# Two thirds of a layer-modulation product moved from TensorE matmuls to VectorE multiply-adds, with a column of ones on TensorE for the sum over partitions

## The reference, cut to what matters

```python
...
"w_mod": n(ks[4], (DEPTH_2, D_MODEL, 3 * D_MODEL), 0.5 * D_MODEL ** -0.5),
"b_mod": n(ks[5], (DEPTH_2, 3 * D_MODEL), 0.02),
...
# per layer: silu(c) @ w_mod + b_mod, split in three of 2048: shift, scale, gate
```

## Time and profile before

| what | value |
|---|---|
| median of 3 runs | 2578.33 us (2578.1 to 2579.03) |
| profiled execution, first to last instruction (its span) | 2577.6 us |
| PE busy | 2556.3 us, 99% |
| DVE busy | 1702.8 us, 66% |
| ACT busy | 1274.2 us, 49% |
| DMA | 570.19 MB, mean 221 GB/s |
| granted TensorE clock | 0.999 of full |

### The profile page before, as it was taken

One profiled execution on the slowest core, in us unless ns is written; L12 is line 12 of the kernel. 1 busy time (PEld: TensorE's weight loads), 2 busy tenths in 40 slices (PEclk: granted clock), 3 DMA queues, 4 the chain that ended last, 5 costly groups with the idle time before them and its releaser, 6 DMA issues.

```text
span 2577.6 us, 31440 instructions
## 1 busy us (share of the span) xinstructions
PE 2556.3 (99%) x12416; PEld 2051.5 (80%) x12416; DVE 1702.8 (66%) x2467; ACT 1274.2 (49%) x1754; POOL 94.9 (4%) x142
## 2 busy tenths in 40 slices
PE   8999999999999999999999999999999999999998
PEld 6777777777777777788888888888888888888887
DVE  5555665664654444457688767598986765898866
ACT  6544544534534333345445565445655554455654
POOL 0000000000000000000100000020000000200000
PEclk9999999999999999999999999999999999999999
DMA  9776786776776777875655447744446666545454
GB/s 336 256 274 229 243 283 229 245 270 227 254 260 222 286 273 278 291 262 198 225 181 178 164 152 259 254 165 164 147 158 221 237 209 216 184 147 164 148 182 177
DMA packets 350594, 570.19 MB, mean 221 GB/s; under 512 B 18208, under 2 KB 202784, under 8 KB 346608
## 3 DMA queue, kind: packets, MB, share of 16 engines
q1 hardware_dynamic: 343216, 532.84, 60.3%
q0 software_dynamic: 6512, 34.60, 3.8%
q10 hardware_dynamic: 720, 0.75, 0.1%
HBM read 559.70 MB, written 8.42 MB: 220 GB/s over the span
## 4 chain that ended last, share of the span: by engine, by line
PE 95%; DMA 3%; ACT 1%; DVE 1%; issue 0%; POOL 0%; SPq 0%; DVEq 0%; ACTq 0%
PE acc L454 28%; PE acc L456 27%; PE acc L455 27%; PE aux L889 3%; PE aux L1094 2%; PE aux L1119 1%; DMA raw<-in_w_o 1%; PE aux L1236 1%; DMA raw<-in_w_mod 1%; PE aux L1104 1%; DMA xr_s<-c_mid 1%; DMA xr_s<-x_mid 1%; PE aux L751 1%; PE aux L1013 0%; PE aux L1074 0%; PE aux L766 0%
## 5 line engine op out<-in xcount | busy, mean ns | idle before, releaser
L442 DVE TENSOR_TENSOR w_lo<-raw,w_hi 128x1024 fp32r<-128x1024 f32 x808 | 993.3, 1233 | 730.9 <-ACT w_hi L434 730.1
L434 ACT ACTIVATE w_hi<-raw 128x1024 fp32r<-128x1024 f32 x808 | 848.6, 1059 | 909.9 <-PE acc L456 888.7
L454 PE MATMUL acc<-w_hi,h_hi 128*128 128x512 f32 x2240 | 892.6, 398 | 10.1 <-DVE w_lo L442 10.1
L456 PE MATMUL acc<-w_hi,h_lo 128*128 128x512 f32 x2240 | 874.3, 390 | 0.0
L455 PE MATMUL acc<-w_lo,h_hi 128*128 128x512 f32 x2240 | 873.3, 390 | 0.0
L454 PEld LDWEIGHTS acc<-w_hi,h_hi 128*128 128x128 f32 x2240 | 421.2, 188 | 124.6 <-issue 32.5
L456 PEld LDWEIGHTS acc<-w_hi,h_lo 128*128 128x128 f32 x2240 | 420.9, 188 | 89.7
L455 PEld LDWEIGHTS acc<-w_lo,h_hi 128*128 128x128 f32 x2240 | 421.6, 188 | 83.4
L454 PE MATMUL acc<-w_hi,u_hi 128*128 128x512 f32 x800 | 318.7, 398 | 0.4 <-DVE w_lo L442 0.4
L456 PE MATMUL acc<-w_hi,u_lo 128*128 128x512 f32 x800 | 312.1, 390 | 0.0
L455 PE MATMUL acc<-w_lo,u_hi 128*128 128x512 f32 x800 | 311.8, 390 | 0.0
(11 more groups left out here) (333 smaller groups left out, 1827.9 us busy)
## 6 DMA issues: line engine op xcount, KB each, us to landing
raw<-in_w_in SPq DMA_DIRECT2D x631, 512.0 KB, 4.5
raw<-in_w_mod SPq DMA_DIRECT2D x192, 512.0 KB, 7.3
raw<-in_w_out SPq DMA_DIRECT2D x96, 512.0 KB, 4.7
raw<-in_w_rnn_out SPq DMA_DIRECT2D x32, 512.0 KB, 5.3
raw<-in_w_o SPq DMA_DIRECT2D x32, 512.0 KB, 5.8
raw<-in_w_attn_out SPq DMA_DIRECT2D x16, 512.0 KB, 4.9
xr_s<-x_mid POOLq DMA_DIRECT2D x4, 1024.0 KB, 12.1
xo<-x_mid POOLq DMA_DIRECT2D x4, 1024.0 KB, 7.9
```

Source lines behind the costliest of these rows:

```text
L434: act.activation(w_hi[:, n % NSPLIT], raw[:, slot, (n % 2) * SK:(n % 2) * SK + SK], ACT.Copy).then_inc(hi_ready, 1)
L442: dve.tensor_tensor(w_lo[:, n % NSPLIT], raw[:, slot, (n % 2) * SK:(n % 2) * SK + SK], w_hi[:, n % NSPLIT].bitcast(F32), ALU.subtract).the ...
L454: pe.matmul(acc[pair][m][:, :], a_hi[:, k0 + k, tok], w_hi[:, s, k], start=b, stop=False)
L456: last = pe.matmul(acc[pair][m][:, :], a_lo[:, k0 + k, tok], w_hi[:, s, k], start=False, stop=e)
```

## The change

Of the six groups only two, (layer 1, shift) and (layer 0, gate), stay as they were on PE (`PARTS`, 32 tiles, from granules 16 and 80). The other four are cut into halves of 1024 columns, eight of them (`HALVES`), each in eight tiles of 256 rows x 1024 columns (1 MB again, 64 tiles). DVE multiplies a 128 x 1024 piece with one condition value (a column of `smod`) and adds it to an accumulator of 128 x 1024, in place (`mod_row`). Six halves have two values, so 32 operations each; the last two (gate of layer 1, for the tokens alone) have one value, so 16 each: 224 operations, 14 of them the first of their accumulator (a plain multiply). They stand behind the `w_lo` of the granules in a hand-written list (`CALM`). When a half is done, PE multiplies its accumulators by a column of ones, which sums the 128 partitions: four matmuls of 512 columns (two in the last two halves) into partitions 0, 32, 64, 96 of `X[3]` (`mod_half`). Halves 0 to 2 are worked off in part one (granules 15 to 194), 3 and 4 in 221 to 331, half 5 in x0 (509 to 535), half 6 in c1 (644 to 673), half 7 in x1 (678 to 697). Halves 2 to 4 come through the ring `raw`; the five others have buffers of their own, whose loads stand in SP's queue between those of the pairs and wait for DVE's count `mod_rows`.

```diff
-GROUPS = ((0, 0), (0, 1), (1, 0), (1, 1), (0, 2), (1, 2))
...
+CALM += [X0 + n for n in sorted(spans((5, 9), (11, 18), (20, 31), (21, 21), (23, 23), (27, 31)))]
+CALM += [C1 + n for n in (4, 5, 7, 8, 10, 11, 13, 14, 17, 18, 20, 21, 29, 30)] + [X1, X1 + 1]
...
+SUMS = [("part", 0, 58), ("half", 0, AT[0][-1] + 2), ("part", 1, 122), ("half", 1, AT[1][-1] + 3), ("half", 2, AT[2][-1] + 3)]
+SUMS += [("half", h, AT[h][-1] + 2) for h in range(3, 8)]
...
+        def load_own(sp, item):
...
+            if own_before(item) is not None:
+
+                sp.wait_ge(mod_rows, rows_after(h, own_before(item)))
...
+            def mod_half(e, h):
+
+                sums_free(e)
+                pe.wait_ge(mod_rows, OPS_BEFORE[h + 1])
+                values = HALVES[h].values
+                for j in range(2):
+                    for v in range(values):
+                        r = 32 * (values * j + v)
+                        last = pe.matmul(X[3][r:r + 1, :], ones, rows[h][v][:, CH * j:CH * (j + 1)], start=True, stop=True)
+                last.then_inc(mod_sums, 1)
...
+            def mod_row(h, tile, i):
...
+                dve.wait_ge(*landed(("half", h, tile)))
...
+                if k == 0:
+                    i = dve.tensor_scalar(dst, src, smod[:, k, v:v + 1], None, ALU.mult)
+                else:
+
+                    dve.wait_ge(mod_rows, done + 1 - x.values)
+                    i = dve.scalar_tensor_tensor(out=dst, in0=src, scalar=smod[:, k, v:v + 1], in1=dst, op0=ALU.mult, op1=ALU.add)
+                i.then_inc(mod_rows, 1)
...
+            def gate_add(e):
...
+                for j in range(strips):
+                    r = slice(32 * j, 32 * j + values)
+                    i = dve.tensor_tensor(gaterows[g][r, :], X[3][r, :], gaterows[g][r, :], ALU.add)
...
             def mod_sides(n):
...
+                for h, tile, i in OPS_AT[n]:
+                    mod_row(h, tile, i)
+                for e, (_, _, at_granule) in enumerate(SUMS):
+                    if n == at_granule + 4:
+                        gate_add(e) if IS_GATE[e] else chunk_copy(e)
+                    if n == at_granule + 8 and not IS_GATE[e]:
+                        columns_read(e)
```

More of the change, by code:

```diff
@@ new lines @@
+CALM += [X1 + n for n in (6, 8, 11, 12, 13, 14, 15, 16, 17, 18, 20, 21, 22, 23, 24, 25)]
+Half = namedtuple("Half", "layer part half values slots first")
+HALVES = [
+    Half(0, 0, 0, 2, (0, 1) * 4, 15),
+    Half(0, 0, 1, 2, (0, 1) * 4, 74),
+    Half(0, 1, 0, 2, None, 136),
+    Half(0, 1, 1, 2, None, 216),
+    Half(1, 1, 0, 2, None, 0),
+    Half(1, 1, 1, 2, (0, 1) * 4, X0),
+    Half(1, 2, 0, 1, (0, 1, 0, 1, 0, 2, 2, 2), C1),
+    Half(1, 2, 1, 1, (0, 1) * 4, X1),
+]
+HOLD = 4
+AT, free = [], 0
@@ new lines @@
+for x in HALVES:
+    many, at_granules = 2 * x.values, []
+    free += sum(n < x.first for n in CALM[free:])
+    while len(at_granules) < many * HALF_TILES:
+        tile = CALM[free:free + many]
+        if x.slots or tile[-1] - tile[0] <= HOLD:
+            at_granules += tile
+            free += many
+        else:
+            free += 1
+    AT.append(at_granules)
+PARTS = [(1, 0), (0, 2)]
+PART_AT = [16, 80]
+SUMS = [("part", 0, 58), ("half", 0, AT[0][-1] + 2), ("part", 1, 122), ("half", 1, AT[1][-1] + 3), ("half", 2, AT[2][-1] + 3)]
@@ new lines, with group @@
+SUMS += [("half", h, AT[h][-1] + 2) for h in range(3, 8)]
+def group(e):
+    kind, i, _ = SUMS[e]
+    return PARTS[i] if kind == "part" else (HALVES[i].layer, HALVES[i].part)
+IS_GATE = [group(e)[1] == 2 for e in range(len(SUMS))]
+COLUMNS_BEFORE = [sum(not g for g in IS_GATE[:e]) for e in range(len(SUMS) + 1)]
+GATES_BEFORE = [sum(IS_GATE[:e]) for e in range(len(SUMS) + 1)]
+GATE_EVENTS = [e for e in range(len(SUMS)) if IS_GATE[e]]
+HALVES_BEFORE = [sum(k == "half" for k, _, _ in SUMS[:e]) for e in range(len(SUMS) + 1)]
@@ new lines @@
+LOADS, taken = [], 0
+BEFORE_PAIR = [[] for _ in range(GRANULES // 2 + 1)]
+for i, first in enumerate(PART_AT):
+    for m in range(KT):
+        BEFORE_PAIR[(first + 6 * (m // 2)) // 2].append(("part", i, m))
+for h, x in enumerate(HALVES):
+    for t in range(HALF_TILES):
+        first = AT[h][2 * x.values * t]
+        start = first - 2
+        if x.slots:
+            clear = AT[h][2 * x.values * (max(t - 2, 6 * (h == 6 and t == 7)) + 1) - 1] if t >= 2 else {0: 12, 1: AT[0][-1], 5: X0 - 2, 6: C1 - 8, 7: X1 + 3}[h]
+            start = min(max(first - 6, clear + 6), first)
+        BEFORE_PAIR[start // 2].append(("half", h, t))
@@ new lines, with own_slot, own_queue, own_before @@
+for p in range(GRANULES // 2):
+    LOADS += BEFORE_PAIR[p]
+    for i in range(taken, min(p + LEAD + 1, GRANULES // 2)):
+        LOADS.append(("pair", i))
+        taken = i + 1
+RING = [item for item in LOADS if item[0] != "half" or not HALVES[item[1]].slots]
+PLACE = {item: n for n, item in enumerate(RING)}
+OWN = [item for item in LOADS if item not in PLACE]
+def own_slot(item):
+    return HALVES[item[1]].slots[item[2]]
+def own_queue(item):
+    return min(own_slot(item), 1)
+def own_before(item):
+    _, h, i = item
+    return max([t for t in range(i) if own_queue(("half", h, t)) == own_queue(item)], default=None)
@@ new lines, in slot_of, with load @@
+        def slot_of(item):
+            return PLACE[item] % NLOAD
+        def load(sp, place, pieces):
+            slot = place % NLOAD
+            if place >= NLOAD:
+                kind, i, *tile = RING[place - NLOAD]
+                if kind == "pair":
+                    sp.wait_ge(lo_ready, 2 * i + 2)
+                elif kind == "part":
+                    sp.wait_ge(mod_used, KT * i + tile[0] + 1)
+                else:
+                    sp.wait_ge(mod_rows, rows_after(i, tile[0]))
@@ L404, in two_ranges @@
             return pieces
[L406 to L420, removed]
         def hi(act, q, n, fresh=False):
-            place = q.place(n // 2)
-            slot = place % NLOAD
+            pair = "pair", (q + n) // 2
+            slot = slot_of(pair)
             if n == 0 and fresh:
```

441 lines of the change are left out of this document (268 added, 173 removed).

## The result

| | before | changed |
|---|---|---|
| median | 2578.22 us (2576.98 to 2579.03, 4 runs) | 2543.14 us (2541.07 to 2545.93, 4 runs) |
| span of the profiled execution | 2577.6 us | 2539.3 us (its time: 2541.07 us) |

The ratio is 0.9863, 95% interval 0.9852 to 0.9875.

A forecast was written before the change was run, and what follows sets the result against it. PE, busy 99% of the span, was taken as the bound. Terms: -61.4 + 6.7 + 1.1 + 12.3 + 0.9 + 1 = -39.4 us from 2577.6, so 2538.2; median 0.7 above, 2539 us, range 2529 to 2555.

The forecast's parts named there:

- The 32 pairs: Modulation matmuls on PE: 64 of 96 tiles go, 1.92 us a pair, -61.4 us.
- The sums: Eight sums added to PE at 0.96 us each, seven of them counted: +6.7 us, bounds 2.5 to 10.
- Half 5's sum: In stream x0: falls where PE waits anyway, so it was left out of the cost.
- DVE's operations: 210 multiply-adds at 1.20 us and 14 multiplies at 0.7: 262 us added, DVE some 1959 us busy, no bound.
- Part one: Part one and branches, halves 0 to 4: 160 operations, 190 us, hidden by DVE's lead of nearly 6 us; counted 0.
- Stream x0: Half 5, granules 529 to 536: DVE overfull beside taps and POOL's windows, `w_lo` late for PE, +12.3 us.
- the second half of the contention: Stream x0: slowing by POOL's windows formerly paid from DVE's lead, now before 536's `w_lo`: 4.1 us, or 2.8.
- x1's gates: Two gate adds of 0.69 us at granule 703, before x1's windows, against a lead of 0.46: +0.9 us.
- Loads and SP's queue: Part of the loads come later and SP's `mod_rows` waits hold back pair loads: +1 us, 0 to 6.
- Rival 3: Slower: SP held at 40 own-buffer tiles; at 1.0 us each all gain gone, at 2 us 2619; chance 0.04.
- Rival 2: Loads bind: late tiles hold DVE and all `w_lo`, 17 to 34 us, 2556 to 2573 us; chance 0.08.
- rival 1: Backlog in x0 much smaller, below 3 us, about 2522 to 2529 us; chance 0.08.

The follow-up runs named there:

- the second experiment: Changed kernel with the twelve GpSimd window operations of stream x0 cut to two columns each: 2537.34 us, ratio 0.9838.
- the first experiment: Changed kernel with 30 of half 5's 32 multiply-adds working on 32 of 1024 columns, loads and waits kept: 2532.19 us, ratio 0.9822.
- the three edits: Changed kernel with half 5 earlier in x0, x0's taps four granules later, halves' ring tiles loaded two granules later: together 2526.91 us, ratio 0.9801.
- the best version: Changed kernel with half 5 earlier, x0's taps later and halves' ring tiles loaded later, all in one kernel: 2526.91 us, ratio 0.9801.

## Why the prediction was right, step by step

**PE as the bound: right.** Work taken off it came back one for one. **The 32 pairs: right in kind, too small.** -61.4 was said, -65.6 came. The step that was mis-sized is "2.15 us, of which 0.23 is the step": it ended at the start of the next matmul, and left out the 0.11 to 0.13 that this one loses. **The sums: too small.** 0.96 was said, 1.06 + 0.13 came; the guess that a lone batch pays its changeover in full was nearer (1.3). Half 5's sum was said to hide in PE's wait; it stands behind the last wait and costs its 1.2 like the others. Together +9.5 for +6.7. These two errors nearly cancel (-4.2, +2.8), which is luck. **Transposes**: +1.1 said, +1.3 came.

**DVE's operations: right.** 1.20 a step was said; 2.39 for two was measured, 1.195 each. DVE's busy time came to 1946, not 1959. The timeline of two in a row, outside the windows:

```profile
1609.05 2.47 DVE L2142 SCALAR_TENSOR_TENSOR rows_u<-rows_in,smod,rows_u 128x1024 f32<-128x1024 f32 x2
1611.44 1.21 DVE L575 TENSOR_TENSOR w_lo<-raw,w_hi 128x1024 fp32r<-128x1024 f32 x1
```

**Part one: right**, no wait for `w_lo` there; from 57 to 1106 us DVE went from 563 to 761 us busy and PE stayed full but for granule 239 and the tile at 28.

**Stream x0: right in place, cause and size.** +12.3 was said, 12.2 came, at the granules named. Within it a part was read too low and another too high: I took 3.5 us for the second half of the contention (12.3 - 8.8), between 2.8 and 4.1. DVE lost 8.1 in all, as before, so the whole second half of 4.1 counts. The Trainium skill's rule (SBUF — State Buffer, "Who interferes with whom") would have kept that 4.1; the measured 8.1 agrees with it in DVE's loss, though POOL's work also grew from 15.5 to 19.5 us. What remains without the windows is 4.0 (the second experiment), where the sum had 8.8 - 4.0 = 4.8.

**The clock: missed.** It cost 1.5 us in x0 in the profiled run and 0 to 2.7 in others. My sum held waits of PE of 4 us and more and no thought of what they do to its clock. The rows that I had read gave 1.00, but PE's timeline of the kernel before shows it: ten matmuls at 0.43 us behind the first wait of 10.12 us, some 2 us lost.

**x1's gates: wrong, small.** +0.9 was said, nothing came: the difference doesn't move behind granule 703.

**Loads and SP's queue: +1 said, +2.8 came**, at one place that I had not named. Rival 3 ("each of the 40 tiles with buffers of their own holds SP") described what happens: SP waited for DVE's multiply-adds 22 times at such tiles, 61.6 us in all and at most 8.6, and PE shows none of it. What cost time was one wait at the ring, behind a tile of half 3. Its price of 1.0 us a tile was never near. Rival 2 is excluded by the first experiment, rival 1 by the waits themselves.

**Profile and median.** The sum is made for a profile, and -39.4 stands against -38.3. That it is off by 1.1 us and no more is luck in part: its single terms are off by 12 us in all, up and down. The other 3.1 us of the miss are the step from span to median. I had set 0.7 for it, from before; after, the median lies 3.9 above the span. In every execution whose span is on record the time is 1.8 or 1.9 us more than the span, so the profiled execution of before (2577.6) was slower than its median by about 1.1, and the changed one (2541.07) was faster than its by 2.1. The medians alone fell by 35.1 us. Eight single times of the changed kernel spread over 7 us (2541.07 to 2548.24), nine of the kernel before over 2.3 on one chip (2577.47 to 2579.76) and 4.0 on another (2577.88 to 2581.87). The clock in x0 (0 to 2.7 us) and at granules 239 and 240 (0 to 1.6), the slow matmuls at the start (1.1) and the waits for tiles (1.5 to 3.3) differ between the profiles by about as much; which of them made a given timed run longer was not seen.

## What to carry to other kernels

When work goes from a full engine to one that is two thirds busy, its total there says little: find the stretch where that engine already has a second stream of work and another engine that slows it, and lay the new operations ahead of it, as far as the buffers let them stand; by the medians the two edits that did this were worth 11 of the 16 us that the three edits gained. Measure an interruption on the full engine up to where its rhythm is restored, two steps on, not to the first instruction behind it. An early load into a shared ring is not free: it holds the ring, and the in-order queue behind it, until its reader is done. And look at what the full engine does behind each wait, not only at the wait: here the clock added 0 to 2.7 us.

## What the runs showed of the hardware

- The granted clock of TensorE fell to 0.50 after an idle time of 4.7 us in the middle of a program that otherwise ran near 1.00. Matmuls of 512 columns then stepped 0.43 us instead of 0.23, and whether that cost anything depended on whether the next wait swallowed it. It also fell behind shorter waits, of 2.1 us (half 5 earlier, granule 534), and behind one of 2.5 us at granule 239 in five profiles of ten: the same wait cost 2.6 to 2.8 or 4.2 to 4.4 us.
- Small fp32 matmuls of 128 x 128 step 0.23 us each, as much as one of 512 columns in the products here (34 took 7.8).
- DVE and POOL, both reading SBUF, slow each other for as long as both run: DVE lost 8.1 us before and after, 7.7 in the best version, POOL's twelve operations took 15.5 to 19.5 us by what DVE ran beside them, single operations of 1.2 us up to 3.12.
- A sum over 128 partitions by a column of ones cost 1.06 us for four float32 matmuls of 512 columns in four strips, 1.05 for two, and the interruption 0.13 more.
